# LayerNorm pieces issued one at a time around the PV evacuations, and the third conv group ahead of the next block's Q/K

## What is computed

```python
x = layer_norm(x, ln0_g, ln0_b)
q, k, v, z_a, bg, cg, h, z_c = jnp.split(x @ w_in, 8, axis=-1)
y_att  = chunk_attention(heads(q), heads(k), heads(v), rel_bias) * silu(z_a)
y_conv = bg * causal_depthwise_conv3(cg * h) * silu(z_c)
x = layer_norm(ALPHA * x + concat(y_att, y_conv) @ w_out, ln_g, ln_b)
```

## Time and profile before

| | |
|---|---|
| median of 3 runs | 1482.41 us (1480.38 to 1483.36) |
| the profiled execution: its time, span of its slowest core (core 5) | 1481.46 us, 1479.9 us |
| spans of the 8 cores, their mean granted TensorE clock | 1472.5 to 1479.9 us, 0.972 to 0.977 |
| TensorE matmul, VectorE, ScalarE, GpSimd busy (core 5) | 92%, 68%, 46%, 26% |

### The profile page before, as it was taken

How to read it: one execution, slowest core, us unless ns; L and a number is a source line. 1 busy time by engine, 2 the same in 40 slices (tenths; PEclk the granted TensorE clock), 3 DMA queues, 4 the chain that set the end, 5 groups by cost and what they waited for, 6 DMA issues and landing times.

```text
span 1479.9 us, 28855 instructions; the slowest of 8 cores (1472.5 to 1479.9 us)
## 1 busy us (share of the span) xinstructions
PE 1359.7 (92%) x9504; PEld 640.6 (43%) x9504; DVE 1002.6 (68%) x1507; ACT 683.1 (46%) x1045; POOL 385.9 (26%) x656
## 2 busy tenths in 40 slices
PE   4979799999999999999999999989999999999994
PEld 2334344444444444444444444444444444444441
DVE  4577776667676775766667676675767667575466
ACT  3334454554533555454543544455453454545550
POOL 4650312222221222223222122222222122221222
PEclk9989999999999999999999999999999999999997
DMA  8971322212122221212212222221212212121011
GB/s 283 302 206 49 82 69 79 79 23 76 63 85 72 79 66 36 76 61 80 79 27 74 69 76 72 69 59 51 76 63 79 79 49 65 54 78 44 23 51 64
DMA packets 125425, 117.23 MB, mean 79 GB/s; under 512 B 103136, under 2 KB 103136, under 8 KB 125152
## 3 DMA queue, kind: packets, MB, share of 16 engines
q1 hardware_dynamic: 125280, 115.40, 26.3%
HBM read 57.69 MB, written 33.55 MB: 62 GB/s over the span
## 4 chain that ended last, share of the span: by engine, by line
PE 70%; DVE 13%; issue 7%; POOL 4%; DMA 2%; ACT 2%; DVEq 1%; POOLq 0%; SPq 0%; ACTq 0%
PE mm L517 34%; PE mm L623 14%; PE mm L530 12%; PE sc L686 5%; PE pv L733 4%; DVE stats L402 3%; PE sc L697 2%; POOL rstd L409 2%; DVE acc L607 2%; DVE xs L455 1%; POOL rstd L412 1%; DVE gate L560 1%; ACT tz L558 1%; DVE ubuf L596 1%; DVE xs L629 1%
## 5 line engine op out<-in xcount | busy, mean ns | idle before, releaser
L517 PE MATMUL mm<-xnT,w_in_sb 128*128 128x512 bf16 x3072 | 754.3, 387 | 25.9 <-DVE tz L581 4.6
L517 PEld LDWEIGHTS mm<-xnT,w_in_sb 128*128 128x128 bf16 x3072 | 287.4, 99 | 338.1 <-issue 80.2
L707 ACT ACTIVATE PT<-sc 128x768 bf16<-128x768 f32 (+1 forms) x336 | 284.9, 878 | 226.1 <-PE sc L697 117.0
L623 PE MATMUL mm<-w_out_sb,yT 128*128 128x512 bf16 x1024 | 246.8, 383 | 6.2 <-DVE xs L629 4.4
L530 PE MATMUL mm<-w_in_sb,xnT 128*128 128x512 bf16 x1024 | 243.7, 381 | 3.2 <-POOL w_in_sb L380 2.6
L733 PE MATMUL pv<-vA,PT 128*128 128x65 bf16 x2240 | 196.6, 195 | 53.0 <-DVE ynorm L742 52.3
L733 PEld LDWEIGHTS pv<-vA,PT 128*128 128x128 bf16 x2240 | 147.2, 98 | 172.5 <-issue 73.6
L749 POOL TENSOR_TENSOR ytok<-ynorm,gate 128x256 bf16<-128x256 f32 x120 | 111.0, 925 | 412.6 <-DVE ynorm L742 397.9
L607 DVE SCALAR_TENSOR_TENSOR acc<-ubuf,cst_sb,acc 128x512 f32<-128x512 f32 x128 | 100.2, 783 | 64.8 <-ACT acc L599 54.7
L530 PEld LDWEIGHTS mm<-w_in_sb,xnT 128*128 128x128 bf16 x1024 | 94.7, 98 | 111.9 <-issue 14.2
L623 PEld LDWEIGHTS mm<-w_out_sb,yT 128*128 128x128 bf16 x1024 | 95.7, 98 | 107.0 <-issue 17.1
(11 more groups left out here) (63 smaller groups left out, 1157.2 us busy)
## 6 DMA issues: line engine op xcount, KB each, us to landing
xs<-x SPq DMA_DIRECT2D x64, 512.0 KB, 3.8
out<-xs SPq DMA_DIRECT2D x64, 512.0 KB, 2.8
xs<-w_in SPq DMA_DIRECT2D x16, 512.0 KB, 9.6
g1bc_sb<-w_in SPq DMA_DIRECT2D x6, 512.0 KB, 9.7
b1bc_sb<-w_in SPq DMA_DIRECT2D x5, 512.0 KB, 9.2
vA<-w_in SPq DMA_DIRECT2D x5, 512.0 KB, 7.6
yT<-ytok SPq DMA_TRANSPOSE x128, 2.3
xs<-rtab SPq DMA_DIRECT2D x1, 1024.0 KB, 8.3
```

Of the source, the lines that this page charges most:

```text
L517: P.op("pe", lambda e, i=i, kc=kc: e.matmul(mm[i][:, :], lhsT=w_in_sb[:, kc, c0:c0 + 128], rhs=xnT[:, sl, kc, :], start=(kc == 0), stop=(k ...
L623: P.op("pe", lambda e, i=i, c=c: e.matmul(mm[i][:, :], lhsT=yT[:, c, t * 128:(t + 1) * 128], rhs=w_out_sb[:, c, hf * 512:(hf + 1) * 512], ...
L707: P.op("act", lambda e, x=x, j0=j0, w=w: e.activation(out=PT[:, :, OFF[j0]:OFF[j0] + w], in_=sc[x][:, :, 0:w], func=AF.Exp, scale=0.125), ...
```

## The change

Three things are altered. `bg_step` no longer issues an overdue item whole: it issues overdue pieces one at a time, before others, as soon as the planner's estimate of VectorE's backlog is at most 1.0 us (0.1 us for pieces that are not overdue), also in quiet ranges; only 12 positions after the deadline is the rest of an item forced out. `ln0_plan` splits a tile's LayerNorm into three items with releases and deadlines of their own (statistics; `ln0_res_a`; `ln0_res_b` with the cast). In blocks after the first, the third conv group now stands ahead of the first two Q/K pairs (block 1 had that order already), and the numbers that go with it are moved: the casts of tiles 0 and 1 of the next block from positions 4 and 20 to 24 and 40, the plans of tiles 2 and 3 to later deadlines, the stores of the third and fourth output tile a little earlier.

```diff
     def bg_step(force=False):
         now = pos_now[0]
-        for it in [it for it in bgl if it[1] <= now or force]:
+        for it in [it for it in bgl if it[1] + 12 <= now or force]:
             while it[2]:
                 it[2].pop(0)()
             bgl.remove(it)
-        while P.dve_free <= P.clk + 0.1:
-            if any(a <= now <= c for a, c in quiet):
-                return
+        while True:
+            calm = not any(a <= now <= c for a, c in quiet)
             it = min((it for it in bgl if it[0] <= now), key=lambda it: it[1], default=None)
-            if it is None:
+            if it is None or P.dve_free > P.clk + (0.1 if it[1] > now else 1.0) or not (calm or it[1] <= now):
                 return
             it[2].pop(0)()
...
-        if b > 1:
-            units += conv[0] + conv[1] + qk[0] + conv[2] + qk[1] + conv[3] + qk[2] + za + qk[3]
-        elif b == 1:
+        if b:
             units += conv[0] + conv[1] + conv[2] + qk[0] + qk[1] + conv[3] + qk[2] + za + qk[3]
...
-            fns = [lambda: ln0_stats_k(bb, t, 0), lambda: (ln0_stats_k(bb, t, 1), ln0_aggr(bb, t)),
-                   lambda: ln0_res_a(bb, t), lambda: ln0_res_b(bb, t)]
-            if act:
-                fns[3] = lambda: (ln0_res_b(bb, t), late(3, lambda: ln0_act(bb, t)))
-            bgq(base[0] + 8 * u0, base[0] + 8 * u1, fns)
+            bgq(base[0] + 8 * u0, base[0] + 8 * u1 - 12,
+                [lambda: ln0_stats_k(bb, t, 0), lambda: (ln0_stats_k(bb, t, 1), ln0_aggr(bb, t))])
+            bgq(base[0] + 8 * u0 + 3, base[0] + 8 * u1 - 6, [lambda: ln0_res_a(bb, t)])
+            bgq(base[0] + 8 * u0 + 8, base[0] + 8 * u1,
+                [lambda: (ln0_res_b(bb, t), act and late(3, lambda: ln0_act(bb, t)))])
...
-                outs = ((4.3, 7), (6.3, 9), (15, 24), (17, 26))
+                outs = ((4.3, 7), (6.3, 9), (14, 22), (16, 24))
...
-                    at(4, lambda: ln0_act(nxt, 0))
-                    at(20, lambda: ln0_act(nxt, 1))
-                ln0_plan(b + 1, 2, 11, 15.5, True)
-                ln0_plan(b + 1, 3, 13, 17.5, True)
-            ln0_plan(b + 2, 0, 31, 39.5)
-            ln0_plan(b + 2, 1, 33, 39.9)
+                    at(24, lambda: ln0_act(nxt, 0))
+                    at(40, lambda: ln0_act(nxt, 1))
+                ln0_plan((b + 1, 2), 11.5, 17.5, True)
+                ln0_plan((b + 1, 3), 13.5, 20, True)
+            ln0_plan((b + 2, 0), 30, 40)
+            ln0_plan((b + 2, 1), 32.5, 41.5)
```

More of the change, by code:

```diff
@@ L881, in block, with ln0_plan @@
             quiet.append((base[0] + z + 1.35 * S - 2, base[0] + z + 1.35 * S + 3.5))
-        def ln0_plan(bb, t, u0, u1, act=None):
+        def ln0_plan(tile, u0, u1, act=None):
+            bb, t = tile
             if bb >= nblk:
                 return
-            fns = [lambda: ln0_stats_k(bb, t, 0), lambda: (ln0_stats_k(bb, t, 1), ln0_aggr(bb, t)),
-                   lambda: ln0_res_a(bb, t), lambda: ln0_res_b(bb, t)]
-            if act:
-                fns[3] = lambda: (ln0_res_b(bb, t), late(3, lambda: ln0_act(bb, t)))
-            bgq(base[0] + 8 * u0, base[0] + 8 * u1, fns)
+            bgq(base[0] + 8 * u0, base[0] + 8 * u1 - 12,
[3 more added lines that the diff above has]
+                [lambda: (ln0_res_b(bb, t), act and late(3, lambda: ln0_act(bb, t)))])
         def out_plan(t, u0, u1):
@@ L927, in block @@
             if b == 1:
[L928 to L931, removed]
+                ln0_plan((2, 0), 1.3, 12, True)
+                ln0_plan((2, 1), 6.3, 14, True)
+                ln0_plan((2, 2), 11, 18.5, True)
+                ln0_plan((2, 3), 13, 20.5, True)
             else:
                 if nxt is not None:
-                    at(4, lambda: ln0_act(nxt, 0))
-                    at(20, lambda: ln0_act(nxt, 1))
-                ln0_plan(b + 1, 2, 11, 15.5, True)
-                ln0_plan(b + 1, 3, 13, 17.5, True)
-            ln0_plan(b + 2, 0, 31, 39.5)
-            ln0_plan(b + 2, 1, 33, 39.9)
+                    at(24, lambda: ln0_act(nxt, 0))
[4 more added lines that the diff above has]
+            ln0_plan((b + 2, 1), 32.5, 41.5)
         run_units(units)
```

## The result

The changed kernel takes 1424.35 us, the median of 4 runs, against 1482.85 us for the kernel before in the same comparison: a ratio of 0.9607, 95% interval 0.9588 to 0.9626. The prediction was 1421 us (1407 to 1446). The profiled execution took 1423.62 us, with a span of 1422.1 us on its slowest core (core 1), 57.8 us less than before; the sum of the prediction's terms was 61.

What follows compares the result with a forecast made beforehand. TensorE's matmul stream (92% busy) plus its stops and clock was taken as the bound. Evacuation 25, clock 19, last gates 10, blocks 4, 8, 12 5, block 1 4, less 2 for moves: 61 us off 1481.5, forecast 1421 us (1407 to 1446).

Steps and rivals of the forecast that it cites:

- The evacuation: Second head pair's first two tiles, ten blocks: TensorE's loss falls from 3.6 to 1.1 us, 25 us gained in all.
- The clock: Stretches round the evacuation, blocks 2 to 14: 19 us come back if the remaining waits are short enough.
- the rival, that the clock falls after the waits that are left: Thirteen blocks: low clock still follows the remaining waits, costing 22 us of the gain, so 1443 us; chance 0.16.
- The last gates: Place B, ten blocks: loss falls from 1.4 to 0.4 us, 1.0 us gained each, 10 in all.
- The first Q: Fourth tile's chain, 8.0 us, just meets 8.0 us of TensorE work; 2 us charged over thirteen blocks.
- The rival of the late tile: Transposed tile arrives late at the first Q, 1.8 us in each of thirteen blocks, so 1444 us; chance 0.14.
- blocks 4, 8 and 12: Evacuation wait of 2.41 us shrinks, the 0.93 us at the first Q may stay: 1.6 us each, 5 us.
- Block 1: Conv group already there; splitting the item alone is to free its longest wait of 4.39 us: 4 us gained.

Runs made afterwards that it cites:

- The runs with repeats: Changed kernel with one, two or four extra statistics instructions ahead of the second head pair's evacuation in ten blocks: 1432.53, 1452.11 and 1474.78 us.
- the run with pieces alone: Changed kernel with the old order of units and old numbers, keeping piecewise issue and the LayerNorm in three items: 1495.45 us, ratio 1.0064.
- the two repeats: Changed kernel with the fourth tile's first statistics instruction issued two more times ahead of the reciprocal in ten blocks: 1452.11 us, ratio 0.9784.
- the run with the order alone: Kernel before with the third conv group ahead of the first two Q/K pairs, items still whole, old releases and deadlines: 1482.36 us, ratio 0.9963.

## Why the prediction was right, and where it was not

**The evacuation: right.** 1.1 us were to be left, by a walk along ScalarE and VectorE; 1.06 are left in most blocks, 1.4 in block 7. (The walk's own times, 712.6 less 711.4, make 1.2 and not 1.1, a slip of 1 us over ten blocks; the 12 us down in the range are 11 by its own bounds.) The walk's hardest step, L581's start 4.8 us after the scores, came out at 4.80. Only the reciprocal went otherwise in block 7, where `ynorm` followed it after 0.62 us instead of 0.28.

**The clock: right.** 19 us were to return. The mean granted clock rose from 0.973 to 0.985, which is 1479.9 x 0.027 = 40.0 us lost before and 1422.1 x 0.015 = 21.3 after: 18.7. That is a net figure. By stretches of 20 us blocks 2 to 14 gave back 21 us, and block 1 lost some 3 more than before. The rows behind the 19 us are also those of a core with eight falls in ten; the other cores had four to eight, and over all eight cores the mean clock rose from 0.9745 to 0.987, which makes 19 us as well. The runs with repeats show that this hung on the length of the stops: the rival, that the clock falls after the waits that are left, fell. The Trainium skill's rule (page "TensorE: Matmul & The Clock Gate", section "A second HAM failure mode: psum-queue depth-cycling"), that small idle times between groups of matmuls make the clock swing, is not borne out here by short waits: 26 for `ynorm`, of 0.2 to 1.3 us, stand between 224 and 1350 us of the changed kernel, and the clock reads 1.00 throughout. They come once in some 43 us, though, so this says nothing of such waits in close succession. That section gives no length of the idle time; here it was mostly single stops of 2.5 us and more that brought the low clock.

**The last gates: right.** 0.4 us were to be left by start times, and 0.55 are, with one wait of 0.38. **The first Q: right**, and for its reason. It was walked as 8.0 us of chain against 8.0 us of cover; the ordinary blocks show no wait there but one of 0.36 us in block 10 and one of 0.54 in block 5, which the row puts down to ScalarE. In the run with pieces alone that cover is missing, and the wait is there. The rival of the late tile, 1.8 us in thirteen blocks, came true in three: 1.63, 1.49 and 1.60 us in blocks 4, 8 and 12. I had left a wait there in the sum.

**Block 1: wrong.** The step was "splitting the item alone is to free its longest wait of 4.39 us: 4 us". That wait went, and those of 3.27 and 1.23 us nearly so, but one of 6.90 us came at the first Q. The evacuation had not been what bound block 1. VectorE has four tiles' LayerNorm to do there, the other blocks two at this point, and the lumps had only settled where the lateness showed: with items issued whole but the new numbers block 1 waits 3.2 us at a conv unit and 4.2 at the evacuation, and in the two runs with pieces and the old numbers it waits 5.5 and 5.4 us at the first Q. By rows of core 1: up to the evacuation of block 2 the sum had 4 + 1.0 + 2.5 = 7.5 us, and 3.8 came from block 1's output projection on (3.4 to 6.0 on the eight cores, each against itself), so on most cores nearly all of block 1's 4 us are missing. Between blocks 2 and 14 the sum had 53.5, and 51.9 came. The last 1.5 us, behind block 14, the sum had as nothing; they were not followed up.

**Something the prediction did not say** though its numbers used it: that neither half pays alone. It priced the order as a cost (2 us at the first Q) and credited the pieces with the gain. The runs show that without the order the pieces lose 0.6%, and without the pieces the order gains 0.4%.

## What to carry to other kernels

A wait that the profile shows at one place can hide a second chain that is late by nearly as much; before clearing the first, walk the next consumer (here the first Q) with the first wait taken out. Background work in an in-order queue should go out in pieces as small as its instructions, since a lump that waits for another engine holds up everything behind it, wherever its deadline puts it. Stops of TensorE of a few microseconds cost more than their length where the low clock follows them, as it did here, so the wait's own row tells too little: the two repeats above cost 1.7 times the length that they added.

## What the runs showed of the hardware that was not expected

Stops of 2.5 us, shorter than the 3.0 us of the kernel before, brought the low clock in ten blocks of ten on the profiled core, while those of 3.0 us had brought it in eight of ten. On all eight cores the difference is larger: 76 of 80 against 49 of 80, and 46 of 80 in the run with the order alone. So the length of a stop is not all that counts. What stands next to it may: a stop of 2.41 us in blocks 4, 8 and 12, with one of 0.9 to 1.2 us some 2 us behind it, was followed by the low clock 24 times of 24 in the kernel before, and the same stop without the second one 6 times of 24 in the run with the order alone. It does not explain why blocks 3 and 14 of the kernel before kept the clock at 1.00, on all eight cores, while blocks 5, 9 and 13 lost it on all eight; that stays open.

The wait of 6.9 us was put down to L607, an instruction whose result the waiting matmul does not read; the DMA's issue time plus its usual landing time pointed to the true releaser, and the same distance of 3.6 us from issue to TensorE's start in block 8 bears it out.
